# An output projection that shares the merges' block, with half of its weights and its first tile split early

## The reference, cut to what matters

```python
proj = jnp.einsum('btne,ned->btnd', o, w_branch)
gate = jax.nn.sigmoid(g_raw.astype(jnp.float32)).reshape(b, t, N_BRANCH, D_MODEL).astype(x.dtype)
y = jnp.einsum('btd,de->bte', jnp.sum(gate * proj, axis=2), w_out)
return x + y, ckv, k_pe, s_new.astype(x.dtype)
...
y_prompt = rmsnorm(xp, g_final)
y_sample = rmsnorm(xs, g_final)
```

## Time and profile before

| | us |
|---|---|
| median of three runs | 2060.95 |
| the profiled execution | 2063.01 |
| its span, first to last instruction | 2061.1 |
| TensorE busy in the span | 1879.8 (91%) |
| mean granted clock of TensorE, as a share of 2.4 GHz | 0.967 |

### The profile page before, as it was taken

How to read it: one execution, slowest core, us unless ns; L and a number is a source line. 1 busy time by engine, 2 the same in 40 slices (tenths; PEclk the granted TensorE clock), 3 DMA queues, 4 the chain that set the end, 5 groups by cost and what they waited for, 6 DMA issues and landing times. The chain is left out here.

```text
span 2061.1 us, 31604 instructions
## 1 busy us (share of the span) xinstructions
PE 1879.8 (91%) x13519; PEld 1524.8 (74%) x13519; DVE 775.8 (38%) x1495; ACT 595.6 (29%) x1152; POOL 510.3 (25%) x392
## 2 busy tenths in 40 slices
PE   5998888987999877999978999999999999999798
PEld 4644455556999534666657889989889999999676
DVE  4025455555100413444431455555652115111432
ACT  3020333334111422233311334434342223222221
POOL 0000000004221006745104800000015544454420
PEclk8998999998999998999989999999999999999899
DMA  8002000003111135765122642222124334333322
GB/s 278 0 0 70 6 11 9 3 1 115 44 42 31 41 123 176 268 257 174 47 77 63 181 102 51 51 61 51 43 87 107 79 92 131 93 87 83 128 72 82
DMA packets 188519, 175.96 MB, mean 85 GB/s; under 512 B 47676, under 2 KB 155772, under 8 KB 188252
## 3 DMA queue, kind: packets, MB, share of 16 engines
q1 hardware_dynamic: 165228, 120.76, 19.9%
q0 software_dynamic: 20592, 52.63, 8.5%
q10 hardware_dynamic: 2560, 0.56, 0.2%
HBM read 153.73 MB, written 27.47 MB: 88 GB/s over the span
## 5 line engine op out<-in xcount | busy, mean ns | idle before, releaser
L884 DVE TENSOR_SCALAR sb<-sb 128x1024 int32<-128x1024 int32 (+4 forms) x127 | 98.2, 779 | 319.9 <-DMA sb<-in_w_branch 159.8
L2483 POOL TENSOR_TENSOR weights_low<-sb 128x1536 fp32r<-128x1536 f32 x42 | 147.1, 3502 | 183.2 <-DVE sb L884 183.2
L2573 PE MATMUL ps<-h_high_again,weights_high 128*128 128x272 f32 x688 | 142.3, 288 | 2.0 <-ACT weights_high L2522 2.0
L2573 PE MATMUL ps<-h_low,weights_high 128*128 128x272 f32 x688 | 142.3, 288 | 0.0
L2573 PE MATMUL ps<-h_high_again,weights_low 128*128 128x272 f32 x688 | 142.3, 288 | 0.0
L615 POOL TENSOR_TENSOR sb<-sb 32x1088 f32<-32x1088 f32 x8 | 19.8, 2479 | 392.2 <-ACT sb L626 392.2
L2110 PE MATMUL ps<-h_high_again,recurrence_weights_high 128*128 128x384 f32 (+1 forms) x432 | 105.9, 354 | 5.4 <-ACT recurrence_weights_high L1868 4.2
L2573 PEld LDWEIGHTS ps<-h_high_again,weights_high 128*128 128x128 f32 x688 | 108.3, 188 | 2.2 <-ACT weights_high L2522 2.2
L2573 PEld LDWEIGHTS ps<-h_high_again,weights_low 128*128 128x128 f32 x688 | 108.4, 188 | 0.0
L2573 PEld LDWEIGHTS ps<-h_low,weights_high 128*128 128x128 f32 x688 | 108.3, 188 | 0.0
L2522 ACT CAST weights_high<-sb 128x1536 fp32r<-128x1536 f32 (+1 forms) x44 | 64.3, 1461 | 129.9 <-POOL weights_low L2483 126.5
(11 more groups left out here) (337 smaller groups left out, 4054.3 us busy)
## 6 DMA issues: line engine op xcount, KB each, us to landing
sb<-in_w_in SPq DMA_DIRECT2D x82, 512.0 KB, 4.2
sb<-in_w_branch SPq DMA_DIRECT2D x48, 256.0 KB, 4.5
sb<-in_x_prompt SPq DMA_DIRECT2D x16, 512.0 KB, 6.5
values_by_level<-values POOLq DMA_DIRECT2D x56, 128.0 KB, 3.5
sb<-values_by_level POOLq DMA_DIRECT2D x7, 896.0 KB, 7.7
out<-sb SPq DMA_DIRECT2D x10, 512.0 KB, 2.9
h_high_in_dram<-h_high SPq DMA_DIRECT2D x8, 544.0 KB, 7.0
h_high_again<-h_high_in_dram SPq DMA_DIRECT2D x8, 544.0 KB, 13.1
```

Source lines behind the costliest of these rows:

```text
L884: return nc.vector.tensor_scalar(high.bitcast(I32), x.bitcast(I32), -4096, None, ALU.bitwise_and)
L2483: nc.gpsimd.tensor_tensor(flat(wLowR[slot]), flat(wLow[slot]), flat(wHigh[slot]), ALU.subtract)\
L2573: mm = nc.tensor.matmul(bank(4 * (k % 2) + s, n=HS2), w[:, c, :], x[:, t0:t0 + HS2], start=c == 0 and part == 0, stop=c == DC - 1 and part ...
```

## The change

The output block goes away; its work is written into the merges' block, with no meeting of the engines in between.

- `w_out` is loaded in 16 pieces of 128x512 (256 KB) instead of four loads of 1 MB. Pieces 0 to 7 (chunks 0 to 3) are issued two at a time behind the weight loads of items 28 to 31, into columns of the split activations that only the first half of the merges read. Pieces 8 to 15 are issued when item 46 is done, into the places of weights and activations that are free by then.
- VectorE now makes all low parts of the output projection (no GpSimd in it). It splits tile 0 of `yT` in item 27's turn, one of the pieces 0 to 7 in each turn from 28 to 35, tile 1 and pieces 8 to 11 ahead of `consume(47)`, pieces 12 to 15 and tile 2 behind it. The buffers for tiles of `yT` are two after tile 0, not three, so tile `i` is split when tile `i-2` is projected.
- ScalarE makes the high copies behind its sigmoids, and loads its square-root table after the last sigmoid.
- TensorE goes from item 47 straight to tile 0, and orders a chunk's six matmuls by column half: three products of one half, then three of the other. The stationary operand now changes at every matmul; before, two neighbours shared it.

```diff
+        EARLY = 4
+        early_low = [(2 * c + x) * T for c in range(EARLY) for x in range(2)]
+        early_high = [gate_at + (i if i < 4 else i + 4) * T for i in range(2 * EARLY)]
+        late_low = [chunk_at[0] + D * i for i in range(DC - EARLY)]
+        late_high = [w_high_at[1] + D * i for i in range(3)] + [w_low_at[1]]
...
+        FIRST_PIECE = ITEMS + 4
+        def pieces_at(k):
+            return [k - FIRST_PIECE] if FIRST_PIECE <= k < FIRST_PIECE + 2 * EARLY * 2 else []
...
+                def output_weights(p):
+                    c, x = p // 2, p % 2
+                    sp.dma_start(wo[c][x], w_out[0][128 * c:128 * c + 128, 512 * x:512 * x + 512]).then_inc(s_wo[c][x], 16)
                 for k in range(ITEMS + 4, 2 * ITEMS):
                     load(k)
+                    if k == ITEMS + 4:
+                        sp.wait_ge(s_bp, ITEMS)
+                    for p in range(2 * (k - ITEMS - 4), 2 * (k - ITEMS - 4) + 2):
+                        if p < 2 * EARLY:
+                            output_weights(p)
+                sp.wait_ge(s_bp, 2 * ITEMS - 1)
+                for p in range(2 * EARLY, 2 * DC):
+                    output_weights(p)
...
             def _(dve):
+                def output_weights(p):
+                    c, x = p // 2, p % 2
+                    dve.wait_ge(s_wo[c][x], 16)
+                    masked(woHigh[c][x], wo[c][x]).then_inc(s_om, 1)
+                    dve.wait_ge(s_om, p + 1)
+                    nc.vector.tensor_tensor(woLowR[c][x], wo[c][x], woHigh[c][x], ALU.subtract).then_inc(s_ol2, 1)
+                def split_y(i):
+                    if i == 1:
+                        dve.wait_ge(s_bp, 2 * ITEMS - 1)
+                    elif i == 2:
+                        dve.wait_ge(s_bp, 2 * ITEMS)
+                    else:
+                        dve.wait_ge(s_y, i - 2 + 1)
...
                 for k in range(ITEMS + 2, 2 * ITEMS):
+                    if k == 2 * ITEMS - 1:
+                        split_y(1)
+                        for p in range(2 * EARLY, 2 * DC - 4):
+                            output_weights(p)
                     consume(k)
                     if k + 3 < 2 * ITEMS:
                         prepare(k + 3)
+                    if k == ITEMS + 3:
+                        split_first()
+                    for p in pieces_at(k):
+                        if p < 2 * EARLY:
+                            output_weights(p)
+                for p in range(2 * DC - 4, 2 * DC):
+                    output_weights(p)
+                split_y(2)
...
             def _(act):
                     gate_ready(k)
+                    if k == ITEMS + 4:
+                        for i in range(2):
+                            act.wait_ge(s_yl, i + 1)
+                            nc.scalar.copy(y0HighR[i], y0High[i]).then_inc(s_yh, 1)
+                    for p in pieces_at(k - 1):
+                        if p < 2 * EARLY:
+                            output_weights(p)
...
+                act.wait_ge(s_gs, gates_through(2 * ITEMS - 2))
+                nc.scalar.activation(small[:, 40:41], sg[0][:, 0:1], ACT.Sqrt)
+                split_y(1)
+                for p in range(2 * EARLY, 2 * DC):
+                    output_weights(p)
+                split_y(2)
...
-        with nc.Block() as block:
...
             def _(pe):
+                def output(i):
                     r = tile_rows[i]
+                    if i == 0:
+                        pe.wait_ge(s_yh, 2)
+                        pe.wait_ge(s_gs, gates_through(2 * ITEMS - 2))
+                    else:
+                        pe.wait_ge(s_yh, i + 2)
+                    if i == 1:
+                        pe.wait_ge(s_bt, 2 * ITEMS - 1)
                     if i >= 2:
                         pe.wait_ge(s_res, i - 1)
-                    pe.wait_ge(s_yh, i + 1)
                     for c in range(DC):
-                        if i == 0:
-                            pe.wait_ge(s_oh, c + 1)
-                        for part, (y, w) in enumerate(((high, woHighR[c]), (low, woHighR[c]), (high, woLowR[c]))):
-                            for half in range(2):
+                        for x in range(2):
+                            if i == 0:
+                                pe.wait_ge(s_oh, 2 * c + x + 1)
+                            for part, (y, w) in enumerate(((high, woHighR[c][x]), (low, woHighR[c][x]), (high, woLowR[c][x]))):
```

More of the change, by code:

```diff
@@ L2319, in build @@
         s_ba = sem("branch_summed")
+        EARLY = 4
[3 more added lines that the diff above has]
+        late_high = [w_high_at[1] + D * i for i in range(3)] + [w_low_at[1]]
+        wo = [[Arena(early_low[2 * c + x], WORDS).take(512) for x in range(2)] for c in range(EARLY)]
+        wo += [[Arena(at + 512 * x, WORDS).take(512) for x in range(2)] for at in late_low]
@@ new lines, in build @@
+        woHigh = [[Arena(early_high[2 * c + x], WORDS).take(512) for x in range(2)] for c in range(EARLY)]
+        woHigh += [[Arena(at + 512 * x, WORDS).take(512) for x in range(2)] for at in late_high]
+        woLowR = [[rounded(f"output_weights_low{c}{x}", early_low[2 * c + x], 1, 512)[:, 0, :] for x in range(2)]
+                  for c in range(EARLY)]
+        woLowR += [[rounded(f"output_weights_low{EARLY + i}{x}", at + 512 * x, 1, 512)[:, 0, :] for x in range(2)]
+                   for i, at in enumerate(late_low)]
@@ new lines, in build @@
+        res = [Arena(after_small + D * i, WORDS).take(D) for i in range(3)] + [Arena(w_high_at[0] - 512, WORDS).take(D)]
+        sqr = Arena(w_high_at[0] + 512, WORDS).take(D)
+        assert after_small + 3 * D <= w_low_at[1] and w_low_at[1] + D <= w_high_at[0] - 512
+        assert w_high_at[0] + 512 + D <= w_high_at[1]
+        xr = [Arena(chunk_at[17] + D * i, WORDS).take(D) for i in range(2)]
+        gfin = Arena(chunk_at[17] + 2 * D, WORDS).take(D)
+        NTT = TILES + 1
+        x_tiles = [x_prompt[0, 128 * i:128 * i + 128, :] for i in range(TILES)] + [x_sample.rearrange("b t d -> (b t) d")]
@@ L2476, in _ @@
                         prepare(k + 3)
+                    if k == ITEMS + 3:
[6 more added lines that the diff above has]
+                split_y(2)
+                dve.wait_ge(s_gf, 16)
+                for i in range(NTT):
+                    if i >= 1 and i + 2 < NTT:
+                        split_y(i + 2)
+                    r = tile_rows[i]
+                    dve.wait_ge(s_xr[i % 2], 16 * (i // 2 + 1))
+                    dve.wait_ge(s_y, i + 1)
+                    if i >= 4:
+                        dve.wait_ge(s_yst[i % 4], 16 * (i // 4))
+                    nc.vector.tensor_tensor(res[i % 4][0:r], ps[0:r, 1024 * (i % 2):1024 * (i % 2) + D], xr[i % 2][0:r],
+                                            ALU.add).then_inc(s_res, 1)
+                    if i:
+                        finish(i - 1)
+                finish(NTT - 1)
             @block.gpsimd
@@ L2615, in _ @@
                     branch_product(k)
[L2619 to L2636, removed]
@@ L2775, in _ @@
+                        for x in range(2):
+                            if i == 0:
+                                pe.wait_ge(s_oh, 2 * c + x + 1)
+                            for part, (y, w) in enumerate(((high, woHighR[c][x]), (low, woHighR[c][x]), (high, woLowR[c][x]))):
+                                mm = nc.tensor.matmul(bank(2 * (i % 2) + x, r), y, w, start=c == 0 and part == 0,
+                                                      stop=c == DC - 1 and part == 2)
                     mm.then_inc(s_y, 1)
+                for i in range(NTT):
+                    output(i)
```

218 lines of the change are left out of this document (96 added, 122 removed).

## The result

The changed kernel takes 2043.75 us (median of 4 runs, 2042.10 to 2045.92) against 2061.06 us (4 runs, 2060.31 to 2061.39) of the kernel before: a ratio of 0.9912, 95% interval 0.9897 to 0.9926. It is faster, by 17.3 us in these runs. The forecast was 2041.4 us with a range of 2040.6 to 2044.4. The profiled execution took 2045.92 us, the slowest of the four, with a span of 2044.1 us and a mean granted clock of 0.968.

A forecast was written before the change was run, and what follows sets the result against it. TensorE bounds the kernel, with a seam before the output product and a tail behind it. The profiled 2063.01 us less 19.54 for the seam is 2043.47; less 2.06 to the median, 2041.4 us, range 2040.6 to 2044.4.

The forecast's parts named there:

- The seam: From item 47's last matmul to tile 1: 30.71 us holding 11.17 us of work, so closing it saves 19.54 us.
- the order of the matmuls: Output product: changing the stationary operand 432 times, before 216 times, costs 0.
- Early pieces: Splits and casts in turns 27 to 35 beside the merges: cost 0, bounds 0 to 1.36 us a turn, 9 turns.
- The blocked subtraction: Turn 27: VectorE's first subtraction waits for all of GpSimd's, `consume(28)` comes 2.2 us late, 3.9 us are left.
- Late pieces: Eight pieces loaded and split beside item 47, least slack 2.9 us: cost 0, bounds 0 and 3 us.
- The tiles after: Each later tile's split fits in the 11.17 us of the tile before: cost 0, bounds 0 and 0.5 us.
- The last term: End of the sum: the runs' median lies 2.06 us below the profiled execution, carried over from 2043.47 to 2041.4 us.
- the first rival: Tile 0 waits for late pieces, so the seam opens inside: 1 to 3 us, 2042.4 to 2044.4; chance 0.07.
- wait for a late piece: What the first rival claimed in tile 0, if the last piece lands after 1941.3: 1 to 3 us; chance 0.07.
- slip of an item: Merges: ScalarE's cast waiting for an early piece delays later weights, up to 12 us, 2053.6; chance 0.06.
- bound in the tiles after: Later tiles become bound by VectorE and ScalarE: a microsecond over is 7 us in all, 2048.4; chance 0.02.
- pace above 0.233 us: Output product: loads of the stationary operand show, 0.188 us per additional change, 40.6 us more, 2082.0; chance 0.02.

The follow-up runs named there:

- the run in pairs: The changed kernel with the matmul order of the kernel before, two column halves in a row per stationary operand: 2044.71 us, ratio 0.9910.

## Why the prediction was right, and where it was off

*The seam.* Right in mechanism and size. It had 30.71 - 11.17 = 19.54 us. TensorE's first output matmul starts at 1935.58, 0.25 us behind the last row of item 47; tile 0 takes 11.03 us. The block-to-end time fell by 20.1 us (541.9 and 542.0 to 521.8 and 521.9). The other 0.5 us is the pace: 0.2332 us per matmul before, 0.2319 now, over 384 matmuls 0.5 us; the order of the matmuls, priced at 0, has 0.3 of it by the run in pairs, and the rest is open.

*Early pieces.* Right, cost 0. Less the 3.03 us by which all is later, the first tile's split ends at 1764.06 (forecast 1763.98) and the weights' cast of item 30 at 1766.10 (1766.6). The blocked subtraction was forecast as the worst case and is what the trace shows in each turn. The Trainium skill, SBUF — State Buffer, section Who interferes with whom, has such an instruction wait for the whole of the other; the 3.87 us beside GpSimd's 3.62 agree to about 0.2 us. That the slack is real, and ends at or a little below 3 us more in a turn, is shown by the runs with added subtractions; that it ends first at ScalarE's order by the one with the later cast.

*Late pieces.* Right, cost 0. ScalarE had piece 12 at 1939.26 - 3.03 = 1936.2 (forecast 1936.3) and piece 15 at 1942.45 - 3.03 = 1939.4 (1940.1). The slack at piece 15 is 3.5 us, above the 2.9 of the text. The run with all pieces late shows what stands on the other side: VectorE's 1.07 us a piece becomes the bound, 5.3 us.

*The tiles after.* Right, cost 0: one unbroken piece of TensorE.

*The last term.* This one was off. The working took 2.06 us from the profiled execution to the median and gave 2041.4; the median came out at 2043.75, 2.3 us above, though the block gave 0.5 us more than forecast. The step that fails is to treat the stages before the block as fixed, and the 2.06 us from one execution to the median with them (the changed kernel's second profiled execution lay 1.10 us below its median, not above): the length of those stages moves by up to 8 us between executions (1514.74 to 1523.05) and the kernel before alone spreads over 9 us in later runs (2057.96 to 2067.25). Between the two furthest executions 6.2 of the 8.3 us arise where the granted clock was 1.00 in one and 0.98 in the other; of the 3.0 us between the first two profiles only 1.1 do (line 2191 spans 263.9 us before and 265.0 after), and where the rest comes from is open. The three runs before within 0.9 us had made the kernel look steadier than it is, and so the forecast's own range of 2040.6 to 2042.4 was too narrow; the full range held the time only by the room that was left for the first rival, which didn't occur. By ratio, 2041.4 of 2060.95 is 0.9905, inside both intervals (0.9897 to 0.9926, 0.9886 to 0.9918).

*The rivals.* No wait for a late piece, no slip of an item, no bound in the tiles after, and no pace above 0.233 us: all four absent.

## What to carry to other kernels

A seam between two stages is worth what lies between the last instruction of the one and the full pace of the other, idle time, half clock and waits together, and it closes when the next stage's first operands are made in memory that nobody reads any more and in turns where the bound engine doesn't notice. Before adding work to an idle engine, look at what its neighbours have queued behind the result, and keep its turn shorter than the item's: here ScalarE's next cast was late first, and VectorE's turns of 12.7 us against 9.00 made most of the loss. Where stages outside the change drift by more than the change's own details, measure from a fixed instruction inside the trace, and widen the range of the total.

## What the runs showed of the hardware

- A 128x512 subtraction on VectorE that starts beside GpSimd's 128x1536 subtraction lasts 3.87 us against 0.69; GpSimd's own lasts 3.60 to 3.62 us then and 3.49 to 3.51 when VectorE's piece is out of its way. A mask, with one input, is longer too: 1.01 us against 0.42 when it started at 1773.63, with GpSimd's subtraction running to 1774.36.
- 2.5 us of idle TensorE left the granted clock at 1.00; 12.49 us had gone with 0.55 in the stretch behind. With eight more subtractions in a turn, 3.43 us were followed by 0.50; 2.28 us (at 1841.85) by 1.00, and 1.95 us (at 1867.22) by 0.51 within a microsecond. So the length of the last gap alone doesn't decide.
- Matmuls of 128x512 in fp32r run at 0.2319 us each when three in a row go to one bank, and at 0.2327 when two share a stationary operand and alternate banks.
- In thirteen executions the same stages, untouched, took up to 8.3 us more or less to reach the block, with the granted clock at 0.98 or 1.00 in the last 250 us; two executions of the same kernel were up to 3.4 us apart (1522.27 and 1518.87).
